# Reloading ScalarE's function tables less often: one table set for exponential and logarithm, and another order at one layer's entry

## The reference

```python
def rms_norm(x, g):
    y = x * lax.rsqrt(jnp.mean(x * x, axis=-1, keepdims=True) + EPS)
    return y * g
```

```python
z = einsum(q, k) * scale
log_fail = where(mask, log_sigmoid(-z), 0)
later = cumsum(log_fail, reverse=True) - log_fail
a = where(mask, exp(log_sigmoid(z) + later), 0)
o = (a @ v) * silu(gate)
```

## Time and profile before

| | |
|---|---|
| runs | 2599.59, 2598.78, 2594.71 us; median 2598.78 |
| the profiled execution | 2599.46 us, of which the span of the trace is 2597.6 |
| TensorE busy | 2457.4 us (95%) |
| VectorE, ScalarE, GpSimd busy | 1274.6 (49%), 1062.9 (41%), 1015.7 (39%) |
| DMA | 245.5 MB, mean 95 GB/s |
| ACT_TABLE_LOAD | 103 |

### The profile page before, as it was taken

How to read it: one execution, slowest core, us unless ns; L and a number is a source line. 1 busy time by engine, 2 the same in 40 slices (tenths; PEclk the granted TensorE clock), 3 DMA queues, 4 the chain that set the end, 5 groups by cost and what they waited for, 6 DMA issues and landing times.

```text
span 2597.6 us, 31125 instructions
## 1 busy us (share of the span) xinstructions
PE 2457.4 (95%) x11642; PEld 1966.0 (76%) x11642; DVE 1274.6 (49%) x1834; ACT 1062.9 (41%) x1377; POOL 1015.7 (39%) x758
## 2 busy tenths in 40 slices
PE   7999999899999989999988899999999998999999
PEld 5887777788887768777766678888868666788886
DVE  5455567866667661444346562222264444422224
ACT  5435775522222543665546542222253434322222
POOL 3332244444444443212443144444434213344442
PEclk9999999999999999999999999999999999999999
DMA  3221596222222222101221122222212101122221
GB/s 139 77 71 66 194 350 257 106 97 97 97 97 86 78 81 81 49 33 49 97 98 55 44 82 97 97 97 97 97 65 94 57 33 65 51 96 97 96 97 65
DMA packets 35956, 245.50 MB, mean 95 GB/s; under 512 B 3951, under 2 KB 4079, under 8 KB 7188
## 3 DMA queue, kind: packets, MB, share of 16 engines
q1 hardware_dynamic: 30096, 207.12, 22.4%
q10 hardware_dynamic: 5764, 37.06, 3.8%
HBM read 242.06 MB, written 2.11 MB: 94 GB/s over the span
## 4 chain that ended last, share of the span: by engine, by line
PE 62%; issue 15%; DVE 8%; POOL 6%; ACT 5%; DVEq 2%; ACTq 0%; POOLq 0%
PE PS L332 17%; PE PS L338 17%; PE PS L335 16%; POOL WL L286 6%; ACT ARENA L1104 3%; PE PS L432 1%; PE PS L435 1%; PE PS L433 1%; ACT L1104 1%; PE PS L821 1%; DVE LBL L2358 1%; PE PS L1018 1%; PE PS L1030 1%; PE PS L792 1%; PE PS L836 1%
## 5 line engine op out<-in xcount | busy, mean ns | idle before, releaser
L286 POOL TENSOR_TENSOR WL<-WT,WH 128x512 fp32r<-128x512 f32 x754 | 1015.5, 1379 | 1549.3 <-ACT WH L1110 1031.3
L332 PE MATMUL PS<-HH,WH 128*128 128x512 f32 x1568 | 623.2, 397 | 32.0 <-DVE ARENA L1910 7.8
L338 PE MATMUL PS<-HH,WL 128*128 128x512 f32 x1568 | 616.3, 393 | 0.0
L335 PE MATMUL PS<-HL,WH 128*128 128x512 f32 x1568 | 615.6, 393 | 0.0
L1452 ACT CAST WH<-WT 128x2048 fp32r<-128x2048 f32 x90 | 172.1, 1912 | 603.3 <-PE PS L332 603.3
L332 PEld LDWEIGHTS PS<-HH,WH 128*128 128x128 f32 x1568 | 297.8, 190 | 108.6 <-issue 19.5
L338 PEld LDWEIGHTS PS<-HH,WL 128*128 128x128 f32 x1568 | 297.4, 190 | 63.4
L335 PEld LDWEIGHTS PS<-HL,WH 128*128 128x128 f32 x1568 | 297.8, 190 | 60.0 <-issue 0.5
L332 PE MATMUL PS<-YH,WH 128*128 128x512 f32 x840 | 331.2, 394 | 8.0 <-ACT ARENA L1104 3.6
L338 PE MATMUL PS<-YH,WL 128*128 128x512 f32 x840 | 327.3, 390 | 0.0
L335 PE MATMUL PS<-YL,WH 128*128 128x512 f32 x840 | 327.1, 389 | 0.0
(11 more groups left out here) (296 smaller groups left out, 3220.9 us busy)
## 6 DMA issues: line engine op xcount, KB each, us to landing
WT<-weights SPq DMA_DIRECT2D x188, 1024.0 KB, 4.9
ARENA<-w_ada ACTq DMA_DIRECT2D x33, 1024.0 KB, 7.1
ARENA<-w_ada SPq DMA_DIRECT2D x3, 1024.0 KB, 7.6
X<-x_fm SPq DMA_DIRECT2D x4, 512.0 KB, 8.0
out_fm<-X SPq DMA_DIRECT2D x8, 256.0 KB, 2.1
ARENA<-rel_rows ACTq DMA_DIRECT2D x1, 1024.0 KB, 5.3
CON<-constants SPq DMA_DIRECT2D x1, 640.0 KB, 11.5
WT<-weights SPq DMA_DIRECT2D x1, 512.0 KB, 5.0
```

Of the source, the lines that this page charges most:

```text
L286: i = nc.gpsimd.tensor_tensor(WL[s][:, e], WT[s][:, e], WH[s][:, e].bitcast(F32), ALU.subtract)
L332: i0 = nc.tensor.matmul(o, w[0], r[0], start=first, stop=False, skip_group_check=True)
L335: nc.tensor.matmul(o, w[0], r[1], start=False, stop=False, skip_group_check=True)
L338: i2 = nc.tensor.matmul(o, w[1], r[0], start=False, stop=last, skip_group_check=True)
```

## The change

1. Where Exp and Ln are needed, ScalarE loads one set that has both, `natural_log_exp_and_others`, by an explicit instruction in 17 places: `ln_exp_table()`, in place of `ln_ahead()` and in new places ahead of the first Exp or Ln after another function. In the feed-forward parts the next function's table (GELU or Silu) is loaded right after the root. In the built program 41 loads are left.
2. At the stick-breaking entry: 13 raw steps stand ahead of the sums, 7 of the first tile and 6 of the second. VectorE mixes the two accumulators in SBUF, ahead of a single sum for the root; the other sum follows with a semaphore of its own, `first_sum`. The last step's squares are made before the last high part, the low part last. The raw tiles of the second panel go to banks 4 and 5. ScalarE's casts of panels in the loop before stand ahead of k = 1, 3 and 5.

```diff
@@ tensor
-            def norm_sum(second=False):
+            def norm_sum():
...
-                if second:
-                    pe.wait_ge(sem("sq_acc2"), DT - 1)
-                    nc.tensor.matmul(psb(2), ONES, ACC2, start=True, stop=True)
...
             fresh_h()
-            raw_panel(G_SBG, (YH, YL), sums="two")
-            raw_panel(G_SBG + 1, (YH, YL))
+            def raw_steps(g, c, b, k0, k1, opens=False):
+                for k in range(k0, k1):
+                    h_tile(k)
+                    w = wtile(g % 2, DT, 256, k, c, c + P)
+                    i0 = nc.tensor.matmul(psb(b), w[0], YH[:, k, :], start=k == 0, stop=False, skip_group_check=True)
+                    nc.tensor.matmul(psb(b), w[0], YL[:, k, :], start=False, stop=False, skip_group_check=True)
+                    piece(g, k * 256 + c + P)
+                    i2 = nc.tensor.matmul(psb(b), w[1], YH[:, k, :], start=False, stop=k == DT - 1, skip_group_check=True)
...
+            b0, b1 = take(), take()
+            raw_steps(G_SBG, 0, b0, 0, 7, opens=True)
+            raw_steps(G_SBG, P, b1, 0, 6)
+            n["sq"] += DT
+            n["acc"] += DT - 1
+            pe.wait_ge(sem("sq_acc2"), DT)
+            nc.tensor.matmul(psb(2), ONES, ACC2, start=True, stop=True).then_inc(sem("ms_ready"), 1)
+            nc.tensor.matmul(psb(3), ONES, ACC1, start=True, stop=True).then_inc(sem("first_sum"), 1)
+            raw_steps(G_SBG, 0, b0, 7, DT)
+            raw_steps(G_SBG, P, b1, 6, DT)
+            open_pieces(G_SBG + 1)
+            for q in range(2):
+                tiles[0] += 1
+                raw_steps(G_SBG + 1, P * q, SB_AHEAD + q, 0, DT, opens=q == 0)
@@ scalar
-            def ln_ahead():
-                f(COLS[:, 31:32], par("eps"), ACT.Ln)
+            def ln_exp_table():
+                nc.scalar.preload_act_table_set("natural_log_exp_and_others")
...
                 root()
+                nc.scalar.preload_act_table(ACT.Gelu_apprx_tanh if conv else ACT.Silu)
...
                 if conv:
+                    ln_exp_table()
                     for k in range(DT):
                         raw(lambda k: par("norm_ple", k), k, k + 1)
...
             def raw_final(k):
                 fresh(k)
-                f(YH[:, k, :], X[:, k, :], ACT.Copy, scale=COLS[:, 32 + k:33 + k]).then_inc(sem("hh_ready"), 1)
+                if k < DT - 1:
+                    f(YH[:, k, :], X[:, k, :], ACT.Copy, scale=COLS[:, 32 + k:33 + k]).then_inc(sem("hh_ready"), 1)
                 square(X, k)
...
             for k in range(DT):
-                if k and k % 2 == 0:
-                    next_panel(G_PGATE + k // 2)
+                if k in (1, 3, 5):
+                    next_panel(G_PGATE + (k + 1) // 2)
...
             next_panel(G_SBG)
-            act.wait_ge(sem("ms_mix"), 1)
-            f(NRS, NRS, ACT.Ln, scale=1.0 / D, bias=par("eps2"))
+            act.wait_ge(sem("ms_ready"), n["ms"])
+            f(NRS, psb(2), ACT.Ln, scale=1.0 / D, bias=par("eps2"))
             act.drain()
             f(NRS, NRS, ACT.Exp, scale=-0.5).then_inc(sem("root_ready"), 1)
+            act.wait_ge(sem("first_sum"), 1)
             f(FIRST, psb(3), ACT.Ln, scale=1.0 / D, bias=par("eps"))
...
-                free(f(SG[:, k, :], psb(b), ACT.Silu), b)
+                free(f(SG[:, k, :], psb(SB_AHEAD + b if k >= 2 else b), ACT.Silu), b)
...
+            ln_exp_table()
             for q in range(4):
                 v_panel(G_SBV + q, SV, 256 * q)
...
             mla_gate(0)
+            ln_exp_table()
...
+            ln_exp_table()
             next_panel(mlh(0))
             mla_proj(0)
...
-            ln_ahead()
+            ln_exp_table()
             squares(ACC, 6)
             settle(POST_ACC)
             post_root()
@@ vector
             dve.drain()
             final_trail(DT - 1)
+            dve.drain()
+            stt(out=ACC2, in0=ACC1, scalar=EPS, in1=ACC2, op0=ALU.mult, op1=ALU.add).then_inc(sem("sq_acc2"), 1)
+            raw_lo(DT - 1, lambda k: COLS[:, 32 + k:33 + k], (YH, YL))
...
-            dve.wait_ge(sem("ms_ready"), n["root"])
-            nc.vector.tensor_copy(NRS, psb(2))
-            dve.drain()
-            stt(out=NRS, in0=psb(3), scalar=EPS, in1=NRS, op0=ALU.mult, op1=ALU.add)
-            dve.drain().then_inc(sem("ms_mix"), 1)
             dve.wait_ge(sem("root_ready"), n["root"])
             scale()
             scale()
-            normalise(lambda k: COLS[:, 32 + k:33 + k], meanwhile=scale)
-            scale()
+            scale_ahead = lambda: scale(bank=SB_AHEAD)
+            normalise(lambda k: COLS[:, 32 + k:33 + k], meanwhile=scale_ahead)
+            scale_ahead()
```

## The result

| | before | changed |
|---|---|---|
| median of four runs | 2599.11 us | 2576.05 us (2574.88 to 2581.56) |
| ratio | 1 | 0.9919 (95% interval 0.9901 to 0.9937) |
| span of the profiled execution | 2597.6 | 2573.7 |
| ACT_TABLE_LOAD | 103 | 41 |
| ScalarE busy | 1062.9 | 983.4 |

The account below looks back on a forecast made before the run. TensorE was taken to bound the kernel, full in feed-forward loops, so a removed load gains at most the TensorE wait it ends. Terms summed to -38.0 us from 2599.5, 2561.5; with the median 0.7 lower, 2561 us, range 2547 to 2578.

Parts of the forecast that it names:

- the rival of a slower set: Whole kernel: the combined Exp/Ln set is slower per element than the two it replaces, 2611 us and more at twice the duration; chance 0.03.
- point 1: Stick-breaking pairs: TensorE's waits for LBH, L836 and the first LBL go whole, -12.1 us (bounds -8 and -13).
- the 2.2 us for the first LBL of each pair: Stick-breaking pairs: TensorE's wait for the first LBL, 0.27 us in each of 8 pairs, was to go.
- point 2: Latent-attention heads: fewer loads around the 128x8 activation shorten TensorE's waits, -9.0 us (bounds -5 and -13).
- so the 7.5 goes: Latent-attention heads: the activation ends 2 us sooner, so TensorE's 7.5 us of waits at L898 in 6 heads vanish.
- second rival: More than the waits: a switch costs more than its row, or lower-clock stretches go; 2546 us, chance 0.13.
- The 1.5 us that were to come off the waits of L950: Latent-attention heads: the 0.5 us left over per head shortens L950's waits (10.5 in 16), taken as 1.5.
- point 3: Stick-breaking entry: 13 steps ahead of the sums, mixing in SBUF and separate gate banks, -6 us (bounds -3 and -9).
- 4.8 us, which fill idle time: Stick-breaking entry: 21 more matmuls ahead of the sums, 4.8 us, fill TensorE's idle 8.24, of which some 3.5 stay.
- Two gate tiles get banks of their own, so the 3.50 goes: Stick-breaking entry: TensorE's later 3.50 us wait for a bank disappears because two gate tiles use separate banks.
- Differential attention, start, third block, losses: Smaller terms: differential attention -3.3, output gate -1.3, first normalise -1.0, third block -6.5, latent-attention entry +0.2, embedding's gate +1.0 us.
- The first rival: Pairs and heads: the next wait takes over, LBL behind LBH and L950 behind L898; 2578 us, chance 0.22.

## Why the prediction missed its size

- **Loads and their price.** Right: 62 went, each worth 1283 ns of ScalarE, and the rival of a slower set is out. The Trainium skill (ScalarE: Activation LUTs, What ACT_TABLE_LOAD costs) adds a drain of about 1380 ns to each switch. The trace disagrees for this kernel: ScalarE's busy time fell by 79.5 us, and the load that stood on the path when the heads' loads were first put back lengthened the heads by (157.8 - 150.3) / 7 = 1.1 us a head, not 2.7.
- **Pairs** (point 1), -12.1: right in size, -12.6, and the run with the loads back shows that it is the loads. TensorE is at the full clock throughout, 1.00. But the sum behind it came out partly by luck. LBH's 7.8 and L836's 2.1 went, while of the 2.2 us for the first LBL of each pair only 0.4 did (5.5 to 5.1). What made up for it is a term that the sum did not have: TensorE's idle time fell by 10.3 us and its busy time by some 2.4 more, with the same matmuls at the same clock. In the kernel before,

```profile
1399.20 0.39 PE L332 MATMUL PS<-YH,WH 128*128 128x512 f32 x1
1399.43 0.39 PE L335 MATMUL PS<-YL,WH 128*128 128x512 f32 x1
```

  a matmul starts 0.16 us before the one ahead of it ends, and a wait breaks that overlap; 31 waits became 15, so an estimate from these rows is 16 x 0.16 = 2.6 us.
- **Heads** (point 2), -9.0: the step that failed is not "so the 7.5 goes", for it went, but that a wait which goes makes the stretch shorter by its length. That holds near the full clock, where it measures 8.7. The kernel before ran a part of its heads at half clock, and the changed one a larger part; there TensorE's matmuls fill the place of the wait. By the traces the loads are worth 2.1 us there, and the clock's further fall took back 1.7. The prediction had the clock only as an extra gain, in its second rival, with nothing worse against it than that its falls may stay in place; that the clock could fall further, from 21 to 38 us at half speed, was not among the cases. The 1.5 us that were to come off the waits of L950 did not come either (10.5 to 10.4).
- **Entry** (point 3), -6: -0.8. The step that failed is "4.8 us, which fill idle time". Seven steps more ahead of the sums are filling only if they can start early; the two `take()`s in one line put all of them behind the last gate. With the second bank asked for later 1.1 us came back, not 4.8, since the seventh step's `YL` hangs on the last gates too: the filling was put too high even for a free bank. Also "Two gate tiles get banks of their own, so the 3.50 goes" was right for the third tile, and the same 3.50 stood a tile later, ahead of the first normalised one, because of the count. With both mended the entry gave -6.3, at 6.8 us of low clock instead of 10.2, which is worth about 1.7 of it (an estimate, 3.4 us at half speed).
- **Differential attention, start, third block, losses**: the third block -6.9 for -6.5. The first two gave 2.9 of 5.6, with low stretches lying elsewhere. At the latent-attention entry (+2.6 for +0.2) one wait grew from 1.90 to 3.32, as its load was forecast to make it, and others shrank by as much: TensorE is idle for 4.4 us in both. The 2.6 come with 6.8 us at the lower clock, which the kernel before did not have there.
- **The first rival**, the next wait takes over, had its time almost right, 2578, and its mechanism wrong: waits for LBL and L950 did not grow (5.1 and 10.4 against 5.5 and 10.5). What took over in the heads was not a wait but slower work.

Open: why the low stretches of the heads fall as they do. The same heads had 0.93 in one kernel and 0.88 in another with nothing changed in them. And the runs of one kernel differ by up to 11.5 us; one trace of each was read, so the clock's share in a median is known only as far as the trace stands for the runs. Kernels of the table that have the same loads and the same added matmuls agree within 2 us on the heads, which is what the numbers drawn from it rest on.

## What to carry to other kernels

In this kernel a wait of TensorE was worth its length only where TensorE was at its full clock around it: read the granted clock beside the wait, and where it is below 1.00, try a few matmuls without use in the wait that remains together with the removal, since either alone may show little. Count an engine's freed time at zero until the wait that it ends is found, and at an entry where accumulators are taken in turn, look at which bank the first instruction asks for and who frees it, not only at how many there are. When a load of tables is put in by hand, put it ahead of the semaphore wait that it can hide behind, never between the wait and its user.

## What the runs showed of the hardware

- Exp and Ln out of the set that holds both take 1.27 us for 128x1280, as out of their own sets (1.27).
- In the changed kernel's heads the granted clock fell to the lower level in six heads in a row, 1.0 to 2.3 us behind the start of the 16 matmuls of one column, which have a wait of 0.66 us ahead of them. The mean over the heads was 0.87, though TensorE was busy 132.57 of 148 us; with 0.68 us of full-width matmuls per head in that wait it was 0.95.
- The time that a wait costs depends on the clock around it: the same 16 loads came with 0.8 us of waits at the spread matmuls where 41.0 us of the heads were at the lower clock, and with 9.7 us where 10.2 were.
- In this program a bank counts as free by the number of semaphore increments, whoever gives them: a bank free since 921.4 was waited for until 933.6.
